# Moving one small tile and dropping a pad: every on-chip tile of a decoder-layer kernel starts at another byte

## The reference, cut to what matters

```
mod = silu(c) @ w_ada + b_ada                        # shift, scale, gate, twice
h   = rms_norm(x, g_pre_mix) * (1 + sc1) + sh1
u_lru, u_gate, q, k, v, f = split(h @ w_in)          # 2048 x 5128
y_lru = rg_lru(conv4(u_lru)) * gelu(u_gate)
y_att = fox_attention(q, k, v, log_sigmoid(f + b_f)) # 8 heads of 128
y   = concat(rms_norm(y_lru), rms_norm(y_att)) @ w_out   # 2048 x 2048
x   = x + gt1 * rms_norm(y, g_post_mix)
h   = rms_norm(x, g_pre_mlp) * (1 + sc2) + sh2
y   = square(relu(h @ w_ff1)) @ w_ff2                # 2048 x 8192, 8192 x 2048
x   = x + gt2 * rms_norm(y, g_post_mlp)
```

## Time and profile before

| what | value |
|---|---|
| median of 3 runs | 2128.91 us (2127.42 to 2129.04) |
| the profiled execution's own time | 2129.04 us |
| its span, first to last instruction | 2127.3 us |
| TensorE busy, matmuls | 2051.6 us (96%), 9025 records |
| VectorE busy | 1615.4 us (76%) |
| ScalarE busy | 797.5 us (37%) |
| GpSimd busy | 98.9 us (5%) |
| granted TensorE clock, mean | 0.990 |
| moved by DMA | 324.57 MB, 153 GB/s on average |

### The profile page before, as it was taken

How to read it: one execution, slowest core, us unless ns; L and a number is a source line. 1 busy time by engine, 2 the same in 40 slices (tenths; PEclk the granted TensorE clock), 3 DMA queues, 4 the chain that set the end, 5 groups by cost and what they waited for, 6 DMA issues and landing times.

```text
span 2127.3 us, 25152 instructions
## 1 busy us (share of the span) xinstructions
PE 2051.6 (96%) x9025; PEld 1671.2 (79%) x9025; DVE 1615.4 (76%) x1863; ACT 797.5 (37%) x1035; POOL 98.9 (5%) x105
## 2 busy tenths in 40 slices
PE   4999999999999999999999999999999999999997
PEld 4777778788778778888888888888888888888886
DVE  7998597875987887686776776876867867767766
ACT  5324612224553264343343343333333433433433
POOL 1001050000220001000000000000000000000000
PEclk8999999999999999999999999999999999999999
DMA  9975458856437763332333332333223323333333
GB/s 363 380 257 178 139 180 303 289 174 202 139 117 267 262 235 93 116 99 89 108 99 96 119 101 89 108 99 108 98 87 121 99 89 108 99 95 118 103 120 157
DMA packets 181582, 324.57 MB, mean 153 GB/s; under 512 B 12648, under 2 KB 49624, under 8 KB 179216
## 3 DMA queue, kind: packets, MB, share of 16 engines
q1 hardware_dynamic: 173600, 302.08, 43.5%
q0 software_dynamic: 3568, 16.95, 2.2%
q10 hardware_dynamic: 4352, 4.73, 0.7%
HBM read 313.20 MB, written 10.52 MB: 152 GB/s over the span
## 4 chain that ended last, share of the span: by engine, by line
PE 79%; DVE 13%; issue 3%; ACT 3%; DMA 2%; DVEq 0%; SPq 0%; ACTq 0%
PE pair L837 10%; PE pair L835 10%; PE pair L836 10%; PE pair L860 9%; PE pair L862 9%; PE pair L861 9%; PE bank L527 4%; PE bank L528 4%; PE bank L529 4%; PE bank L537 2%; PE bank L539 2%; PE bank L538 2%; DVE acc L1443 2%; DVE w_lo L1415 2%; DVE acc L1473 2%
## 5 line engine op out<-in xcount | busy, mean ns | idle before, releaser
L1863 DVE TENSOR_TENSOR yg<-yg,pair 128x1024 f32<-128x1024 f32 x240 | 289.6, 1217 | 287.5 <-PE pair L862 287.4
L835 PE MATMUL pair<-h_hi,w_lo 128*128 128x512 f32 x1020 | 397.5, 390 | 0.0
L837 PE MATMUL pair<-h_hi,w_hi 128*128 128x512 f32 x1020 | 396.8, 389 | 0.0
L836 PE MATMUL pair<-h_lo,w_hi 128*128 128x512 f32 x1020 | 396.8, 389 | 0.0
L860 PE MATMUL pair<-w_hi,op_lo 128*128 128x512 f32 x840 | 330.1, 393 | 8.9 <-DVE op_lo L1830 8.4
L861 PE MATMUL pair<-w_lo,op_hi 128*128 128x512 f32 x840 | 327.1, 389 | 0.0
L862 PE MATMUL pair<-w_hi,op_hi 128*128 128x512 f32 x840 | 327.1, 389 | 0.0
L965 ACT ACTIVATE w_hi<-raw 128x1024 fp32r<-128x1024 f32 (+1 forms) x114 | 118.4, 1044 | 295.6 <-DMA raw<-in_w_in_dram 175.5
L836 PEld LDWEIGHTS pair<-h_lo,w_hi 128*128 128x128 f32 x1020 | 191.4, 188 | 40.0 <-issue 0.2
L835 PEld LDWEIGHTS pair<-h_hi,w_lo 128*128 128x128 f32 x1020 | 191.5, 188 | 40.0 <-issue 0.2
L837 PEld LDWEIGHTS pair<-h_hi,w_hi 128*128 128x128 f32 x1020 | 191.5, 188 | 39.8
(11 more groups left out here) (272 smaller groups left out, 2769.7 us busy)
## 6 DMA issues: line engine op xcount, KB each, us to landing
raw<-in_w_ada_dram SPq DMA_DIRECT2D x128, 512.0 KB, 4.6
w_raw<-in_w_ff_dram SPq DMA_DIRECT2D x128, 512.0 KB, 3.8
raw<-in_w_ff_dram SPq DMA_DIRECT2D x128, 512.0 KB, 4.5
raw<-in_w_in_dram SPq DMA_DIRECT2D x74, 512.0 KB, 4.6
gst<-in_w_ada_dram SPq DMA_DIRECT2D x64, 512.0 KB, 7.1
raw<-in_w_out_dram SPq DMA_DIRECT2D x32, 512.0 KB, 4.7
x_tok<-in_x_dram SPq DMA_DIRECT2D x4, 1024.0 KB, 8.3
xr<-in_x_dram POOLq DMA_DIRECT2D x4, 1024.0 KB, 7.9
```

The lines of the kernel that those rows point to most:

```text
L835: pe.matmul(b, lo[:, cols], h_hi[:, kt, :], start=(kt == 0), stop=False)
L836: pe.matmul(b, hi[:, cols], h_lo[:, kt, :], start=False, stop=False)
L837: last = pe.matmul(b, hi[:, cols], h_hi[:, kt, :], start=False, stop=(kt == KT - 1))
L1863: dve.tensor_tensor(y, y, pairs[2 + (i + r) % 2][:, :, :], ALU.subtract if i == 6 else ALU.add).then_inc(product_read, 1)
```

## The change

`stat`, 96 floats in each partition, is no longer placed first but behind `A1, S1, A2, S2`. The tile `to_line`, which nothing uses, is gone. The pad ahead of `w1_raw` grows from 352 to 416 floats. No instruction, wait, queue or loop is touched.

```diff
-        stat = sb("stat", [P, 96])
         raw = sb("raw", [P, RING, 2 * COLS])
         w_hi = sb("w_hi", [P, RING, 2 * COLS], F32R)
         w_lo = sb("w_lo", [P, RING, 2 * COLS], F32R)
...
         A1, S1, A2, S2 = (sb(n, [P, KT]) for n in ("A1", "S1", "A2", "S2"))
+        stat = sb("stat", [P, 96])
         lam = sb("lam", [P, 8, CT])
         wf_raw = sb("wf_raw", [P, KT, HEADS])
         bf = sb("bf", [HEADS, 1])
         eps = sb("eps", [P, 1])
         mod = sb("mod", [P, 4])
-        sb("to_line", [P, 56])
...
-            ("pad8", [P, 352], F32), ("w1_raw", [P, 2, 2 * COLS], F32))
+            ("pad8", [P, 416], F32), ("w1_raw", [P, 2, 2 * COLS], F32))
```

## The result

The changed kernel takes 2169.35 us in the median of 4 runs (2168.16 to 2171.3), against 2128.97 us (2127.42 to 2129.63): a ratio of 1.0188, interval 1.0176 to 1.0200. It is 40 us slower, and outside the range that was given.

A forecast was written before the change was run, and what follows sets the result against it. The prediction took the number of fp32r matmuls times their pitch on TensorE to bound the MLP, with VectorE and full DMA engines at the start. All its terms were 0 us, so it forecast 2128.9 us, range 2124 to 2150 us.

The forecast's parts named there:

- What bounds the kernel: In the MLP, time is matmul count times pitch, 0.2265 us each; over the whole kernel 8460 fp32r matmuls, 1916 us.
- the price of the shift on TensorE: On the 8460 fp32r matmuls, shifted operands were taken to cost 0 us, as in the fp32 matmul rows.
- The bound above: Most that each fp32r matmul on TensorE could lose: the convolution's 1.1%, 21 us in all, giving 2150 us.
- TensorE pays for operands off a multiple of 64: Rival for the fp32r matmuls: one cycle more each, 3.5 us, or 1.1%, 21 us; 2132.4 to 2150 us; chance 0.30.
- the rival of a gain: In the MLP, fewer collisions between TensorE's reads and VectorE's and ScalarE's writes: up to 4.6 us faster, 2124.3 us; chance 0.10.
- VectorE and ScalarE: On raw, acc, w1_raw and the convolution, the shift was taken to cost 0, with 0.9 us kept for the start.
- DMA: Loads into the moved tiles were taken to cost 0 us, though no row showed a destination at 32 mod 64.
- The rival of the start: From 0 to 120 us, slower staging transfers, 3.8 us, and the convolution's 0.9: 4.7 us, 2133.6 us; chance 0.08.

The follow-up runs named there:

- stage32: Kernel before, with the staging tiles gst0 and gst1, xnT and the gate weights wrg and wig moved by 32 bytes: 2131.84 us, ratio 1.0011.
- w128: Kernel before, with only stat moved behind S2, to_line and pad8 kept, so weights begin at 128 mod 512: 2158.04 us, ratio 1.0146.
- h64: Kernel before, with to_line cut to 32 bytes, so activations and staging tiles begin at 320 mod 512: 2159.34 us, ratio 1.0141.
- mend: The changed kernel with 96 bytes ahead of the overlays, so weights and activations both begin at 128 mod 256: 2134.22 us, ratio 1.0030.
- raw32: Kernel before, with raw, which TensorE never reads, moved alone by 32 bytes and what lies behind by 512: 2128.89 us, ratio 1.0005.
- all32: Kernel before, with a 32-byte tile behind stat that moves every large tile, weights and activations alike, by 32 bytes: 2133.94 us, ratio 1.0024.
- h32: Kernel before, with only to_line dropped and pad8 at 416, so activations and staging tiles begin at 288 mod 512: 2165.49 us, ratio 1.0173.
- wlo16: Kernel before, with w_lo beginning 16 bytes into its tile: 2151.96 us, ratio 1.0111.

## Why the prediction was wrong

**What bounds the kernel** was right: the MLP's time is the number of matmuls times their pitch, and the pitch is what changed. 5580 matmuls of the MLP at (233.7 - 226.9) = 6.8 ns are 37.9 us; less the 6.6 us of waits for `op_lo` that vanish, 31.3 us, against 29.2 us measured.

**The step that failed** is the price of the shift on TensorE: "I take 0, as the row nearest in kind (same engine, moving and stationary operands shifted by 64 bytes) has it". That row, an fp32 matmul, is near in name only. It starts the next matmul after 428 ns (590 ns busy) where the fp32r matmul of the same shape takes 226.5 (389 busy), so it takes its columns at about half the rate. The two rows did differ in the distance of their operands, 192 mod 256 for `acc` and `ones` and 0 for `hs` and `wrg`, and showed no price, nor did they after the change; on fp32 matmuls only the six records of `stage32` show one, of 5 to 6 ns, and a single record of line 563 or 564 in each of the changed kernel, `w128` and `h64`, 433 to 434 ns. The prediction saw that the fp32r streams were untried and still let the slower kind speak for them.

**The bound above** was too low as well. The convolution's 1.1% comes from VectorE; the pitch rose by 3.0% (6.8 of 226.9 ns), and so the range ended at 2150 us.

**The rival "TensorE pays for operands off a multiple of 64"** named the right engine and the right sign, for a reason that is wrong: all operands off a multiple of 64 cost nothing (1277.0 us), and aligned ones at another distance cost 22 us and more. The idea that counts, that one operand's place relative to another's matters, stood in the rival of a gain, which had the 160 bytes between weights and activations in it; but it looked for the partner among VectorE's and ScalarE's accesses, where moving `raw` shows none, and took the 0.7 us beside pitch and waits as the most that could be at stake. That bounds what can be won from the layout before, not what can be lost.

The rule of the Trainium skill, page "SBUF — State Buffer" (Specifications, the row on cachelines), that lines are of 16 bytes, would have made the change nothing, as every tile moves by a multiple of 32 bytes and so keeps its place in such a line. (The prediction says there that no operand of either kernel begins inside a line; those of the convolution do, 4 to 12 bytes in, before and after alike.) The measurement decides: the time rose by 1.9%.

**VectorE and ScalarE:** 0 was right, off 64 as well (1061 and 1218 ns; line 1472 at 744 instead of 742 ns).

**DMA:** 0 was wrong in the start. The rival of the start had said 4.7 us; moving the staging tiles alone cost 2.7 us, and the mended kernel lost 6.8 us ahead of the MLP. The rule of the Trainium skill, page "DMA: Bandwidth & Descriptors" (How a descriptor splits into AXI transactions), on starts off a multiple of 256 bytes fits the staging tiles: the loads into them landed in 7.1 to 7.8 us at 0 mod 512 and in 7.4 us at 256, and in 9.0 to 9.5 us at 32, 288, 320 and 384. On the loads into `raw` and `w1_raw` it does not show: those of 512 KB landed within 0.2 us of the same time wherever the tiles began, and with `raw` off but not the staging tiles (`w128`, `raw32`) the stretch from 20 to 120 us moved 379 and 380 GB/s, as before. But `raw` seems to add to the staging tiles: with both off (the changed kernel, `all32`, `mend`) the staging loads landed in 9.4 to 9.5 us at 354 to 357 GB/s, and with the staging tiles off but not `raw` (`h32`, `h64`, `stage32`) in 9.0 to 9.2 us at 361 to 363 GB/s.

**Open** are two things. One is why a distance slows the matmuls after it too, and in `wlo16` most of all a pair at a distance of 0; "a stream against the next load" is the best description that the runs give, and not a mechanism that they show. The other is the rest of the loss ahead of the MLP, 6.8 us in the mended kernel against 3.8 us (790.3 - 786.5) with the staging tiles alone. (By the medians it is 6.4 and 2.7; both profiled executions were slower than their medians, by 1.9 and 1.1 us.) In `stage32` 1.6 us are lost by the last staged row, and most of the rest comes between 700 and 800 us, where the clock is 0.95 against 0.97; in `mend` it is 3.1 us, and the lower clock comes from 400 to 500 us. So part of both is clock, and what makes it fall there is not shown. The larger first part goes with `raw` off 256 at the same time, as the landings above do (`all32` has 3.5 us there), but no run had just that pair off.

## What to carry to other kernels

Where TensorE runs fp32r matmuls back to back, give the tiles that it streams and the tiles that it loads as weights the same start modulo 256 bytes, and read the pitch off the timeline before and after any change of layout: here it was worth 3% of every matmul. A small tile or pad placed among large ones can undo that without a single instruction changing. When nothing in a trace shows an operation in the state that a change brings about, a row of a slower kind is not a bound for it.

## What was not expected of the hardware

- fp32r matmuls of 512 columns follow one another more slowly unless the start bytes of streamed and stationary operands agree modulo 256: 226.8 to 226.9 ns from start to start at a distance of 0 (also with every operand at 32 mod 64), 231.5 ns at 16 (`w_lo` alone), 232.2 to 233.7 ns at 32, 64, 96 and 128. The place where the distance is largest suggests a stream against the load of the next stationary operand. fp32 matmuls hardly show it (at a distance of 32, 6 of 16 records took 434 against 429 ns).
- The slowdown carries over: after stationary pieces at a distance of 32, a matmul with all operands at a distance of 0 still takes 230.8 ns to the next start, and the one after it 226.8.
- Loads of 512 KB in rows of 1 KB land in 7.1 to 7.8 us where the rows begin at a multiple of 256 bytes of SBUF and in 9.0 to 9.5 us where they don't, while the DMA engines are full.
